# Three norms of a two-block transformer kernel: a shifted mean, embedding products moved ahead of their gate, and another order of the index projections

## The chip, the cores and the metric

The kernel runs on one core of a Trainium2 chip. The metric is the device time of one execution in microseconds (us), lower is better; shown are the median and the span of three runs. One further execution was recorded by the profiler; all rows below come from it.

## The reference, cut to what matters

Sequence 256 (T), width D = 2048, everything in float32. The first block (adaptive norms, latent attention beside a short convolution, a convolutional feed-forward part) ends in `rms_norm(x, g_final)`. The second block is

```python
def second_block(x, p, ...):
    for i in range(2):
        h = mixer_a(x, ...) if i == 0 else mixer_b(x, ...)
        x = layer_norm(ALPHA * x + h, ln_g[i], ln_b[i])
        x = x + (p[i] @ w_ple[i]) * sigmoid(x @ w_ple_gate[i])
    return x

def layer_norm(x, g, b):
    mu = mean(x)
    var = mean(square(x - mu))
    return (x - mu) * rsqrt(var + 1e-5) * g + b
```

`mixer_a` projects x to q, k, v, a gate, an index query iq (1024 columns), an index key ik (64) and index weights iw (16), chooses keys by the index scores and attends; `mixer_b` is a stick-breaking attention. Both end in a product with an output matrix w_o (2048 x 2048).

## The kernel before

Activations lie transposed: a tile is 128 features x 256 tokens, and the residual `X` is 16 such tiles [128, 16, 256] in SBUF. Weights stream from HBM in chunks of 128 x 2048 floats (1 MB); `schedule()` writes the order of all 342 chunks out by hand, and every engine walks that order. Products are made exact enough by a split in three: ScalarE copies a chunk to a rounded high part (`split(c)` on ScalarE, L376, three `HI` buffers), VectorE subtracts to get the low part (`split(c)` on VectorE, L872), and TensorE does high x high, high x low, low x high (`product`/`chunk`, all recorded under L1664). A chunk is 48 products 128x128x256. Its `HI` buffer is free for chunk c+3 when TensorE has ended chunk c. Four chunks make a group of 512 output columns, which gathers in one of two PSUM tiles `ACC[g % 2]`; a third PSUM tile, `AUX`, takes sums. SyncE issues the chunk loads, five `RAW` buffers ahead.

What the change touches:

- **The final norm of block one** (`n2`). When the last group of the down projection ends (phase `down2`), VectorE adds it to X (`residual`, L1296), ScalarE squares X (`norm_squares`, L621), VectorE sums the squares over the tiles (`part_total`, L996), TensorE sums over the partitions with a matrix of ones (`wide_totals`, into `AUX`), VectorE, ScalarE and VectorE form 1/root (`variance` L1002, `root` L438, L1005), and `normed` (L1026, L1028) with `hi_quarter` (L421) and `lo_quarter` (L1014) makes X and its high and low parts by quarters of four tiles. Then phase `ikw` (2 chunks: index key and weights, 96 products) starts; its loop waits for both parts of all quarters of a chunk. VectorE forms rotation angles (`angles`), ScalarE their sines, both ahead of the split of further chunks. Phase `iq` (8 chunks) follows, then `k_a`, `v_a`, `q_a`, `gate_a`, `o_a`.
- **The layer norms** (`ln0` after `o_a`, `ln1` after `o_b`). `o_a` is 16 chunks. `add_alpha` (L1555) does X = ALPHA X + ACC by group. After the last group: `early_sum`, `last_sum` (L1563, L1570) sum X over tiles, TensorE sums over partitions, VectorE subtracts the mean (L1581), ScalarE squares (L433), VectorE sums (L996), TensorE sums, root, `normed` (L1026, L1029), high and low parts. Then 16 chunks `pgate{i}`, whose groups ScalarE reads with Sigmoid into `U` (L514).
- **The embedding** (`ple{i}`): two chunks, four groups, 96 products, after the gate. VectorE multiplies U by each group (L1606) and, when all four are done, adds U to X by quarters (L1611). After `ple0` X is split again (L421, L1014) for `k_b`; after `ple1` X is stored in four DMAs (L323).

The feed-forward norm `nf` of block one is already done in another form: the squares of tiles 0 to 11 are summed early, those of the last four go straight to the ones product tile by tile, and scale and root are one instruction per tile (L1272, L613, L1278).

Of the kernel before, what the change touches and what calls it, by code (L numbers as in the profile page):

```python
# [13 lines left out]
P = 128  # L14
T = 256
# [47 lines left out]
def schedule():  # L63
# [93 lines left out]
def two_blocks(nc, stream, ada_stream, vecs, consts, x_t, ctx_t, p_t, positions, out):  # L157
# [60 lines left out]
    SEL = place("selector", [P, 8])  # L218
    CC = R2[:, :].rearrange("p (k t) -> p k t", t=T)
# [44 lines left out]
    def sem(name):  # L264
        if name not in sems:
# [4 lines left out]
    NORMS = {"nx": (2, 4), "nc": (2, 4), "nkv": (1, 1), "nq": (1, 1), "n2": (2, 4), "ln0": (2, 4),  # L270
             "ln1": (2, 4)}
# [14 lines left out]
    def since(name, n):  # L286
        s, before = step(name)
        return s, before + n

# [18 lines left out]
    with nc.Block() as block:  # L308
# [3 lines left out]
        def _(eng):  # L312
# [8 lines left out]
            for q in range(4):  # L321
                eng.wait_ge(sem("x2_full"), q + 1)
                eng.dma_start(out[:, 4 * q:4 * q + 4, :], X[:, 4 * q:4 * q + 4, :]).then_inc(sem("stored"), 16)  # L323
            eng.wait_ge(sem("stored"), 64)

        @block.gpsimd
        def _(eng):
# [3 lines left out]
            eng.memset(SEL[:, 3:4], 1.0).then_inc(sem("selector"), 1)  # L331

# [37 lines left out]
        def _(act):  # L370
# [245 lines left out]
            def norm_squares(name):  # L616

                end = PH["ikw"][1]
                for before, s in ((1, slice(0, 12)), (0, slice(12, 16))):
                    act.wait_ge(acc_free, end - before)  # L620
                    nc.scalar.activation(Y[:, s, :], X[:, s, :], ACT.Square).then_inc(step(name + "_sq")[0], 1)  # L621

            def norm(name, dst):
                root(name, T)
                hi_of(dst, AH, name + "_full", name + "_hi")

# [45 lines left out]
            def enter2():  # L672
                norm("n2", X)
                act.wait_ge(sem("angles"), 1)

                for i, (cos, sin) in enumerate(((COS2, SIN2), (COSI, SINI))):
                    r = Y[:, i, :]
                    nc.scalar.activation(cos[:, :], r, ACT.Abs).then_inc(sem("abs_angle"), 1)
                    nc.scalar.activation(sin[:, :], r, ACT.Sin).then_inc(sem("tables"), 1)
                for i, cos in enumerate((COS2, COSI)):  # L680
                    act.wait_ge(sem("abs_angle"), 2)
                    nc.scalar.activation(cos[:, :], cos[:, :], ACT.Sin, bias=con("half_pi"), scale=-1.0)\
                        .then_inc(sem("tables"), 1)
            pending[0] = enter2
            c0 = PH["ikw"][0]
            for j in range(2):
                split(c0 + j)
                if j == 0:
                    norm_squares("n2")
                if j == 1:  # L690
                    flush()
            phase("iq", 2)
# [8 lines left out]

            def gate_evac(name, d0, func):

                g0 = PH[name][1]

                def evac(gi):
                    act_evac(g0 + gi, U[:, gi * 4 + d0:gi * 4 + d0 + 4, :], func=func)
                return evac
# [30 lines left out]
            def mixer(tag, k, v, q, gate, early, attend):  # L739
# [3 lines left out]
                split(c0)  # L743
                split(c0 + 1)
                flush()
# [46 lines left out]
            def layer_norm(i):  # L792
                def f():
                    squares(f"ln{i}", X, Y, ready=f"ln{i}_centred")
                    root(f"ln{i}", T)
                    hi_of(X, AH, f"ln{i}_full", f"ln{i}_hi")
                return f

            def embed(i, then):
                phase(f"pgate{i}", 4, evac=gate_evac(f"pgate{i}", 0, ACT.Sigmoid))  # L800
                c0 = PH[f"ple{i}"][0]
                split(c0)
                flush()
                split(c0 + 1)
                pending[0] = then

            phase("o_a", 4, then=layer_norm(0), done=4)
            embed(0, lambda: hi_of(X, AH, "x1_full", "x1_hi"))
# [45 lines left out]
            phase("o_b", 4, then=layer_norm(1), done=4)  # L854
            embed(1, lambda: None)
# [3 lines left out]
        def _(dve):  # L859
# [498 lines left out]

            def angles():
# [16 lines left out]
            def enter2():  # L1376
                dve.wait_ge(acc_free, PH["ikw"][1])
                part_total("n2", 1, 12)

            def final_norm():  # L1380
                variance("n2", T, D, EPS)
                normed("n2", X, X, lambda k: vec("g_final", k), None, "a_ready")
                angles()
            c0, g0 = PH["ikw"]
            last = PH["down2"][1] + 3
            for j in range(2):
                split(c0 + j)
                if j == 0:
                    part_total("n2", 0, 12)
                    residual("down2", 5 * KD)(3)  # L1390
                    enter2()
                else:
                    final_norm()

            def ikw_evac():
                take(g0)
                V.tensor_copy(Y[:, 12, :], ACC[g0 % 2][:, 0, :])
                V.tensor_copy(R0[0:IH, 0:T], ACC[g0 % 2][0:IH, 1, :]).then_inc(acc_free, 1)
                V.engine_nop().then_inc(sem("ik"), 1)
            pending[0] = ikw_evac  # L1400
            phase("iq", 2, evac=copy_out("iq", Y, 4))
# [48 lines left out]
            def early_a(m, gk, gq):  # L1450
                if m == 1:
# [8 lines left out]
                if 2 <= m < 5:  # L1460
                    b = (2, 0, 1)[m - 2]
                    n = 4 if b < 2 else 1
                    turn_pairs(Y[:, 4 + 4 * b:4 + 4 * b + n, :], COSI[:, :], SINI[:, :], PERMI, n, "index_in")
# [47 lines left out]
            def mixer(tag, k, q, gate, out, early, attend):  # L1511
# [14 lines left out]
                split(c0)  # L1526
                split(c0 + 1)
                flush()
# [16 lines left out]
            def by_act(gi):  # L1545
                pass

            def add_alpha(name):
                g0 = PH[name][1]

                def evac(gi):
                    take(g0 + gi)
                    dve.wait_ge(acc_free, g0 + gi)
                    x = X[:, bass.ds(gi * 4, 4), :]
                    V.scalar_tensor_tensor(out=x, in0=x, scalar=ALPHA, in1=ACC[(g0 + gi) % 2][:, :, :],  # L1555
                                           op0=ALU.mult, op1=ALU.add).then_inc(acc_free, 1)
                return evac

            def early_sum(i):
                def f():  # L1560

                    dve.wait_ge(acc_free, PH[f"pgate{i}"][1] - 1)
                    V.tensor_reduce(RSTD[:, T:2 * T], X[:, 0:12, :].rearrange("p k t -> p t k"), AX.X, ALU.add)  # L1563
                return f

            def last_sum(i):
                def f():
                    n = f"ln{i}"
                    dve.wait_ge(acc_free, PH[f"pgate{i}"][1])
                    link(V.tensor_reduce(RSTD[:, 0:T], X[:, 12:16, :].rearrange("p k t -> p t k"), AX.X, ALU.add))  # L1570
                    V.engine_nop().then_inc(sem(n + "_sum"), 1)
                return f

            def layer_norm(i):
                def f():
                    n = f"ln{i}"
                    dve.wait_ge(sem(n + "_mean"), 1)
                    link(V.tensor_scalar(RSTD[:, T:2 * T], AUX[:, 1, 0:T], 1.0 / D, None, ALU.mult))
                    for q in range(4):
                        s = slice(4 * q, 4 * q + 4)  # L1580
                        V.tensor_tensor(X[:, s, :], X[:, s, :], wide_bcast(RSTD[:, T:2 * T], 4), ALU.subtract)\  # L1581
                            .then_inc(sem(n + "_centred"), 1)
                    dve.wait_ge(sem(n + "_centred"), 4)
                    part_total(n, 0, 8)
                    part_total(n, 1, 8)
# [704 lines left out]
```

## Time and profile before

| | us |
|---|---|
| median of 3 runs | 2480.45 |
| lowest, highest | 2479.01, 2482.07 |
| the profiled execution | 2482.17 |
| its span in the trace | 2480.4 |
| mean granted TensorE clock | 0.968 of full |

Busy shares of the span: TensorE 94%, its weight loads 87%, VectorE 61%, ScalarE 40%. The DMA engines moved 190 GB/s on average. The chain of work that ended last lies 82% on TensorE and 11% on VectorE. In a row of the timeline the first number is the start, the second the duration of the merged run of instructions; durations of neighbouring TensorE instructions overlap, since they are pipelined, so the pace of products is read from starts.

### The profile page before, as it was taken

Reading aid. Unit: us, or ns where it says so; the run is one execution under the profiler, and the core shown is the slowest. Engines: PE = TensorE matmul, PEld = TensorE weight load, DVE = VectorE, ACT = ScalarE, POOL = GpSimd, SP = SyncE. Lnnn points to the kernel's source line nnn. Section 1 sums busy time; section 2 is a strip of 40 time slices with the busy share of each in tenths; the row PEclk is TensorE's granted clock in tenths of the full one; section 3 lists DMA queues with packets and bytes.
Section 4 is the critical chain, followed back from the end, with each engine's and each line's share of the span. In section 5 each row is a group of like instructions: output and inputs, shape, how many; then the busy total and the mean of one; then the engine's idle time right before and its main releaser. Section 6 shows DMA issues by size and latency. Waiting matters only on the chain.

```text
span 2480.4 us, 39098 instructions
## 1 busy us (share of the span) xinstructions
PE 2321.6 (94%) x17514; PEld 2157.9 (87%) x17514; DVE 1507.5 (61%) x1652; ACT 993.6 (40%) x922; POOL 59.0 (2%) x111
## 2 busy tenths in 40 slices
PE   6979999998999999999998799999959899999688
PEld 1249878898999999999998799899959899999688
DVE  2167777787877546554566678665474545545664
ACT  1033534434444334443443343445334336653232
POOL 1100000000000000000000000000000000000000
PEclk9989989999999999999999899999979899999899
DMA  9746855685776545554555354334525354335333
GB/s 387 282 159 234 302 224 206 231 315 184 297 264 221 194 179 185 187 183 178 184 187 187 119 183 157 125 127 158 187 85 187 141 185 150 120 138 185 136 136 119
DMA packets 64808, 471.84 MB, mean 190 GB/s; under 512 B 7200, under 2 KB 7200, under 8 KB 8192
## 3 DMA queue, kind: packets, MB, share of 16 engines
q1 hardware_dynamic: 50400, 365.65, 40.4%
q0 software_dynamic: 14096, 101.59, 10.9%
q8 instruction: 138, 2.26, 0.4%
q10 hardware_dynamic: 144, 2.10, 0.2%
q14 instruction: 30, 0.25, 0.0%
HBM read 467.21 MB, written 2.10 MB: 189 GB/s over the span
## 4 chain that ended last, share of the span: by engine, by line
PE 82%; DVE 11%; DMA 2%; ACT 2%; issue 2%; ACTq 0%; POOL 0%; DVEq 0%; POOLq 0%
PE acc L1664 71%; PE aux L1664 10%; DMA ada_raw<-ada_stream 2%; DVE lo L872 2%; ACT hi L376 1%; DVE ada_acc L892 1%; DVE rstd L996 1%; DVE rstd L1005 0%; DVE rstd L1563 0%; DVE x L1581 0%; DVE x L1611 0%; DVE x L1026 0%; DVE rstd L989 0%; PE aux L1854 0%; DVE rope_scratch L1411 0%
## 5 line engine op out<-in xcount | busy, mean ns | idle before, releaser
L872 DVE TENSOR_TENSOR lo<-raw,hi 128x2048 fp32r<-128x2048 f32 x342 | 782.2, 2290 | 699.0 <-ACT hi L376 698.7
L376 ACT ACTIVATE hi<-raw 128x2048 fp32r<-128x2048 f32 x342 | 652.8, 1913 | 840.0 <-PE acc L1664 825.3
L1664 PE MATMUL acc<-act_hi,hi 128*128 128x256 f32 x4464 | 618.9, 290 | 58.4 <-DVE u_lo L1014 18.1
L1664 PEld LDWEIGHTS acc<-act_hi,hi 128*128 128x128 f32 x4464 | 576.2, 196 | 74.7 <-issue 68.6
L1664 PE MATMUL acc<-act_lo,hi 128*128 128x256 f32 x4464 | 599.2, 285 | 4.0 <-DVE act_lo L1014 4.0
L1664 PE MATMUL acc<-act_hi,lo 128*128 128x256 f32 x4464 | 595.4, 283 | 0.0
L1664 PEld LDWEIGHTS acc<-act_lo,hi 128*128 128x128 f32 x4464 | 567.3, 194 | 4.3 <-DVE act_lo L1014 4.3
L1664 PEld LDWEIGHTS acc<-act_hi,lo 128*128 128x128 f32 x4464 | 563.3, 193 | 0.0
L892 DVE SCALAR_TENSOR_TENSOR ada_acc<-ada_raw,silu_c,ada_acc 128x512 f32<-128x512 f32 x224 | 153.7, 746 | 8.1 <-DMA ada_raw<-ada_stream 7.7
L1664 PE MATMUL aux<-ada_raw,silu_c 128*2 128x512 f32 x256 | 113.8, 599 | 20.4 <-DMA ada_raw<-ada_stream 20.4
L1664 PEld LDWEIGHTS aux<-ada_raw,silu_c 128*2 128x2 f32 x256 | 20.8, 85 | 107.0 <-issue 93.3
L1664 PE MATMUL acc<-u_hi,hi 128*128 128x256 f32 x688 | 89.8, 283 | 0.0
L1664 PE MATMUL acc<-u_lo,hi 128*128 128x256 f32 x688 | 89.7, 283 | 0.0
L1664 PE MATMUL acc<-u_hi,lo 128*128 128x256 f32 x688 | 89.7, 283 | 0.0
L1664 PEld LDWEIGHTS acc<-u_lo,hi 128*128 128x128 f32 x688 | 85.7, 192 | 0.0
L1664 PEld LDWEIGHTS acc<-u_hi,lo 128*128 128x128 f32 x688 | 85.7, 192 | 0.0
L1664 PEld LDWEIGHTS acc<-u_hi,hi 128*128 128x128 f32 x688 | 85.7, 192 | 0.0
L639 ACT ACTIVATE y<-acc,vectors 128x256 f32<-128x256 f32 x86 | 41.7, 565 | 79.9 <-PE acc L1664 79.9
L335 POOL DMA_DIRECT2D ada_raw<-ada_stream x96 | 51.1, 533 | 704.5 <-DVE ada_acc L892 588.5
L1312 DVE SCALAR_TENSOR_TENSOR y<-acc,vectors,y 128x255 f32<-128x255 f32 x86 | 35.6, 476 | 49.3 <-ACT y L639 49.3
L1664 PE MATMUL aux<-rstd,ones 128*128 128x256 f32 (+1 forms) x30 | 13.9, 595 | 44.4 <-DVE rstd L996 29.8
L1664 PEld LDWEIGHTS aux<-rstd,ones 128*128 128x128 f32 x30 | 7.4, 279 | 49.1 <-DVE rstd L996 31.4
(297 smaller groups left out, 1616.7 us busy)
## 6 DMA issues: line engine op xcount, KB each, us to landing
raw<-stream SPq DMA_DIRECT2D x342, 1024.0 KB, 4.8
ada_raw<-ada_stream POOLq DMA_DIRECT2D x96, 1024.0 KB, 5.7
x<-x_t SPq DMA_DIRECT2D x1, 2048.0 KB, 9.3
ctx<-ctx_t SPq DMA_DIRECT2D x1, 2048.0 KB, 16.2
x<-x_t ACTq DMA_DIRECT2D x1, 2048.0 KB, 9.0
out<-x SPq DMA_DIRECT2D x4, 512.0 KB, 2.9
p_raw<-p_t POOLq DMA_DIRECT2D x1, 512.0 KB, 4.8
consts<-consts SPq DMA_DIRECT2D x1, 385.5 KB, 19.2
```

The costliest lines, as they stand in the source:

```text
L335: eng.dma_start(ADA[slot][:, :], ada_stream[n]).then_inc(ada_full[slot], 16)
L376: nc.scalar.activation(HI[c % NH][:, :], RAW[c % NR][:, :], ACT.Copy).then_inc(hi_done, 1)
L639: nc.scalar.activation(Y[:, i, :], ACC[(base[0] + gi) % 2][:, t, :], ACT.Identity, scale=VV[:, bass.ds(w + 1, 1)], bias=VV[:, bass.ds(w + ...
L872: V.tensor_tensor(LO[c % NR][:, :], RAW[c % NR][:, :], HI[c % NH][:, :].bitcast(F32), ALU.subtract)\
L892: V.scalar_tensor_tensor(out=a, in0=w, scalar=s, in1=a, op0=ALU.mult, op1=ALU.add)\
L996: ins = V.tensor_reduce(o, src.rearrange("p k t -> p t k"), AX.X, ALU.add)
L1312: ins = V.scalar_tensor_tensor(out=Y[:, i, 1:T], in0=acc[:, t, 0:T - 1], scalar=VV[:, bass.ds(w, 1)], in1=Y[:, i, 1:T], op0=ALU.mult, op1= ...
L1664: return TE.matmul(out, lhs, rhs, start=start, stop=stop, skip_group_check=True)
```

## The change

**Final norm and index projections.** `iq` comes ahead of `ikw` in the schedule. The norm takes the form that `nf` has. Chunks of `iq` start with their own quarter of the high part, and wait for the low part only at their second pass. `angles` and the sines move into `iq`; ScalarE, not VectorE, reads the groups of `iq`; `ikw` is a plain group, read at the start of `k_a`.

**Layer norms and embedding.** `ple{i}` comes ahead of `pgate{i}`. After two groups of `o` a mean over 1024 features is taken as `SHIFT` (two sums, and a product with ones after chunk 8 of `o`) and subtracted; the norm's sums are then taken of the shifted values, as mean and mean of squares, and VAR = E[y^2] - E[y]^2. The sums over partitions stand inside `ple`, after its first 12 products. Product and sum with the embedding are done with each gate group (`finished`), the last group in halves.

The schedule:

```diff
+    wide("iq", "w_in_a_2", 5120, 2)
     phase("ikw")
     group("w_in_a_2", [(6144, 6208), (6144, 6208)] + 8 * [(6208, 6224)], per=8)
-    wide("iq", "w_in_a_2", 5120, 2)
...
     def embed(i):
-        wide(f"pgate{i}", "w_ple_gate_2", 0, 4, layer=i)
         phase(f"ple{i}")
         for g in range(2):
             group("w_ple_2", [(1024 * g, 1024 * (g + 1))], range(2), layer=i, n_groups=2)
+        wide(f"pgate{i}", "w_ple_gate_2", 0, 4, layer=i)
```

VectorE at the final norm (`n2_scaled` is one instruction a tile in the form of L1272; ScalarE's `n2_high` and splits stand in the same order):

```diff
+            n2_scaled(0)
+            n2_scaled(1)
+            n2_low(0)
+            split(c0 + 2)
+            n2_scaled(2)
+            n2_low(1)
+            split(c0 + 3)
+            n2_scaled(3)
+            n2_low(2)
+            n2_low(3)
```

VectorE in the new `embed(i, o, nxt)`; c0 is the first chunk of `o`, so that 16 and 17 are `ple`, 18 to 33 `pgate`:

```diff
+                for n in range(2, 16):
+                    split(c0 + n + 2)
+                    if n in (4, 8):
...
+                        V.scalar_tensor_tensor(out=x, in0=x, scalar=ALPHA, in1=ACC[(go + g) % 2][:, :, :],
+                                               op0=ALU.mult, op1=ALU.add).then_inc(acc_free, 1)
+                        dve.wait_ge(acc_free, go + g + 1)
+                        total_of(RSTD[:, T * g:T * g + T], x, "ln_first")
+                    if n == 9:
+                        dve.wait_ge(*ln(i, "mean", 1))
+                        link(V.tensor_scalar(SHIFT, AUX[:, 0, 0:T], 1.0 / (D // 2), None, ALU.mult))
...
+                scaled(0)
+                scaled(1)
+                low(0)
+                split(c0 + 18)
+                scaled(2)
+                low(1)
+                split(c0 + 19)
+                scaled(3)
+                low(2)
+                low(3)
+
+                for n in range(18, 34):
+                    if n < 32:
+                        split(c0 + n + 2)
+                    elif nxt:
+                        split(PH[nxt][0] + n - 32)
+                    if n in (23, 27, 31):
+                        g = (n - 23) // 4
+                        dve.wait_ge(acc_free, gg + g + 1)
+                        finished(4 * g, 4 * g + 4)
```

Between them, by n: 9 and 10 subtract SHIFT from quarters 0 and 1 (128x1024 each); 10 and 11 form ALPHA X - SHIFT in quarters 2 and 3; 12 adds ACC to quarter 2; 13 sums the squares of tiles 0 to 7 (128x2048), 14 sums X in quarter 2, 15 its squares. Behind the loop ACC is added to quarter 3 in halves; then MEAN, its square, the variance and the reciprocal. `scaled(q)` subtracts MEAN from a quarter and multiplies its four tiles by gain and 1/root; `low` makes the low part tile by tile; `finished(a, b)` multiplies gate by embedding and adds the product and the norm's bias to X.

ScalarE in the same function, behind the root (`high` makes the high part by tiles, `embedded(g)` copies an embedding group to `U` and frees its ACC tile):

```diff
+                embedded(0)
+                high(0)
+                embedded(1)
+                split(c0 + 18)
+                high(1)
+                embedded(2)
+                split(c0 + 19)
+                high(2)
+                embedded(3)
+                high(3)
```

TensorE:

```diff
+                def shift(c):
+                    if c == c0 + 8:
+                        pe.wait_ge(*ln(i, "first", 2))
+                        mm(AUX[:, 0, 0:T], ONES[:, :], RSTD[:, 0:T], True, False)
+                        mm(AUX[:, 0, 0:T], ONES[:, :], RSTD[:, T:2 * T], False, True).then_inc(sem("ln_mean"), 1)
...
+                            if g == g0 and k == 0:
+                                sums()
```

`sums` is 5 products with ones on sums and tiles of X and 6 on sums and tiles of squares. For `k_b` the quarters of X are split as they become final. The output is stored in five DMAs, the last two of two tiles each.

## Rows read from the trace of the kernel before

**Rows 1.** The page, part 1: busy us (share), instructions.

```profile
PE 2321.6 (94%) x17514; PEld 2157.9 (87%) x17514; DVE 1507.5 (61%) x1652; ACT 993.6 (40%) x922; POOL 59.0 (2%) x111
```

**Rows 2.** Waits over the span: us in total, times, longest.

```profile
ACT hi L376 <- PE acc L1664: 825.3, 243, 9.0
DVE lo L872 <- ACT hi L376: 698.7, 241, 10.1
```

**Rows 3.** Timeline, one chunk of o_a: start, us, engine, line, instruction.

```profile
1804.96 2.08 PE L1664 MATMUL acc<-act_hi,hi 128*128 128x256 f32 x16
...
1805.22 1.92 ACT L376 ACTIVATE hi<-raw 128x2048 fp32r<-128x2048 f32 x1 [3.84 <-PE acc L1664]
...
1807.17 2.29 DVE L872 TENSOR_TENSOR lo<-raw,hi 128x2048 fp32r<-128x2048 f32 x1 [3.47 <-ACT hi L376]
```

**Rows 4.** Windows: stretch, length, busy us, PEclk, DMA share, GB/s.

```profile
596.00:601.00 5.00, 2.67 (x13) 1.71 (x11) 2.97 (x6) 1.29 (x3) 0.00 (x0) 1.00 0.59 211
...
1354.60:1373.90 19.30, 2.08 (x5) 1.21 (x5) 17.49 (x27) 7.72 (x7) 0.00 (x0) 0.59 0.16 55
...
1816.50:1846.80 30.30, 4.29 (x10) 2.35 (x8) 25.22 (x19) 6.58 (x5) 0.00 (x0) 0.54 0.09 35
...
2334.20:2364.40 30.20, 4.23 (x9) 2.34 (x8) 25.13 (x18) 6.58 (x5) 0.00 (x0) 0.56 0.10 35
```

**Rows 5.** Timeline around the final norm n2, to the start of k_a.

```profile
1353.00 1.60 PE L1664 MATMUL acc<-u_hi,lo 128*128 128x256 f32 x12
1354.79 1.65 DVE L1296 SCALAR_TENSOR_TENSOR x<-acc,ada,x 128x256 f32<-128x256 f32 x4
...
1385.42 1.28 ACT L679 ACT_TABLE_LOAD   x1
1386.71 0.42 ACT L679 ACTIVATE sin<-y 128x256 f32<-128x256 f32 x1
...
1436.62 2.08 PE L1664 MATMUL acc<-act_hi,hi 128*128 128x256 f32 x16
```

**Rows 6.** Timeline around the norm nf of block one.

```profile
596.90 1.65 DVE L1200 SCALAR_TENSOR_TENSOR x<-acc,ada,x 128x256 f32<-128x256 f32 x4
...
598.48 1.99 PE L1664 MATMUL aux<-y,ones 128*128 128x256 f32 x8 [1.80 <-ACT y L609]
...
603.20 3.25 DVE L1272 SCALAR_TENSOR_TENSOR y<-x,scales,rstd 128x256 f32<-128x256 f32 x8
603.72 3.30 ACT L613 ACTIVATE act_hi<-y,ada 128x256 fp32r<-128x256 f32 x8 [2.34 <-DVE y L1272]
...
605.57 3.75 PE L1664 MATMUL acc<-act_hi,hi 128*128 128x256 f32 x16 [5.10 <-ACT act_hi L613]
...
613.61 2.08 PE L1664 MATMUL acc<-act_hi,hi 128*128 128x256 f32 x16
```

**Rows 7.** Timeline from the end of o_a to the second chunk of k_b.

```profile
1814.56 2.08 PE L1664 MATMUL acc<-act_hi,lo 128*128 128x256 f32 x16
...
1821.68 1.93 DVE L1570 TENSOR_REDUCE rstd<-x 128x256 f32<-128x1024 f32 x1
...
1838.16 2.08 PE L1664 MATMUL aux<-rstd,ones 128*128 128x256 f32 x4 [12.36 <-DVE rstd L996]
...
1841.18 1.75 DVE L1005 RECIPROCAL rstd<-rstd 128x256 f32<-128x256 f32 x1 [0.48 <-ACT rstd L438]
1842.96 1.22 DVE L1026 TENSOR_TENSOR x<-x,rstd 128x1024 f32<-128x1024 f32 x1
...
1846.84 3.40 PE L1664 MATMUL acc<-act_hi,hi 128*128 128x256 f32 x16 [6.61 <-ACT act_hi L421]
...
1970.34 2.08 PE L1664 MATMUL acc<-act_hi,hi 128*128 128x256 f32 x16
```

**Rows 8.** Timeline from the end of o_b to the end.

```profile
2332.20 2.08 PE L1664 MATMUL acc<-act_hi,lo 128*128 128x256 f32 x16
...
2472.25 4.62 DVE L1611 TENSOR_TENSOR x<-x,u 128x1024 f32<-128x1024 f32 x4
```

More of the change, by code:

```diff
@@ L288, in since, with ln @@
         return s, before + n
+    LN_COUNTS = {"sq": 5, "hi": 16, "scaled": 16, "ready": 16, "first": 2, "mean": 1, "centred": 2, "begun": 2,
+                 "part": 3, "last": 2, "sums": 2, "var": 1, "std": 1, "gate": 2}
+    def ln(i, kind, n):
+        return sem("ln_" + kind), i * LN_COUNTS[kind] + n
     raw_full = [sem(f"raw_full{i}") for i in range(NR)]
@@ L614, in _ @@
                     .then_inc(sem("nf_hi"), 1)
[L616 to L625, printed above, removed]
             seen = [0]
@@ L684, in _ @@
[L684 to L692, printed above, removed]
+            c0, g0 = PH["iq"]
+            last = PH["down2"][1] + 3
+            act.wait_ge(acc_free, last)
+            nc.scalar.activation(Y[:, 0:12, :], X[:, 0:12, :], ACT.Square).then_inc(sem("n2_sq"), 1)
+            split(c0)
@@ new lines, in _, with n2_high @@
+            split(c0 + 1)
+            for i in range(2):
+                act.wait_ge(sem("x_summed"), 2 * i + 2)
+                s = slice(12 + 2 * i, 14 + 2 * i)
+                nc.scalar.activation(Y[:, s, :], X[:, s, :], ACT.Square).then_inc(sem("n2_sq"), 1)
+            root("n2", T)
+            def n2_high(q):
+                act.wait_ge(sem("n2_scaled"), 4 * q + 4)
+                nc.scalar.activation(AH[:, 4 * q:4 * q + 4, :], X[:, 4 * q:4 * q + 4, :], ACT.Copy)\
+                    .then_inc(sem("n2_hi"), 1)
@@ L790, in _ @@
             mixer("a", "k_a", "v_a", "q_a", "gate_a", early_a, attend_a)
[L792 to L805, printed above, removed]
@@ L809, in _ @@
+            embed(0, "o_a", "k_b")
             steps3 = [0]
@@ L853, in _ @@
             mixer("b", "k_b", "v_b", "q_bb", "gate_b", lambda m: None, attend_b)
-            phase("o_b", 4, then=layer_norm(1), done=4)
-            embed(1, lambda: None)
+            embed(1, "o_b", None)
         @block.vector
@@ L1357, in _, with n2_scaled, n2_low @@
                             res(g)
+            c0, g0 = PH["iq"]
+            last = PH["down2"][1] + 3
+            dve.wait_ge(sem("n2_sq"), 1)
+            V.tensor_reduce(RSTD[:, T:2 * T], Y[:, 0:12, :].rearrange("p k t -> p t k"), AX.X, ALU.add)\
+                .then_inc(sem("n2_ss"), 1)
+            split(c0)
+            split(c0 + 1)
+            take(last)
+            for t in range(4):
+                k = 12 + t
+                V.scalar_tensor_tensor(out=X[:, k, :], in0=ACC[last % 2][:, t, :],
+                                       scalar=MOD[:, 5 * KD + k:5 * KD + k + 1], in1=X[:, k, :],
+                                       op0=ALU.mult, op1=ALU.add).then_inc(sem("x_summed"), 1)
+            dve.wait_ge(sem("x_summed"), 4)
+            V.engine_nop().then_inc(acc_free, 1)
+            variance("n2", T, D, EPS)
+            def n2_scaled(q):
+                for k in range(4 * q, 4 * q + 4):
+                    V.scalar_tensor_tensor(out=X[:, k, :], in0=X[:, k, :], scalar=vec("g_final", k),
+                                           in1=RSTD[:, 0:T], op0=ALU.mult, op1=ALU.mult).then_inc(sem("n2_scaled"), 1)
+            def n2_low(q):
+                dve.wait_ge(sem("n2_hi"), q + 1)
+                s = slice(4 * q, 4 * q + 4)
+                V.tensor_tensor(AL[:, s, :], X[:, s, :], AH[:, s, :].bitcast(F32), ALU.subtract)\
+                    .then_inc(sem("a_ready"), 1)
             def angles():
@@ L1374, in angles @@
                 V.engine_nop().then_inc(sem("angles"), 1)
[L1376 to L1401, printed above, removed]
+            n2_scaled(0)
+            n2_scaled(1)
+            n2_low(0)
+            split(c0 + 2)
+            n2_scaled(2)
+            n2_low(1)
+            split(c0 + 3)
+            n2_scaled(3)
+            n2_low(2)
+            n2_low(3)
+            for m in range(2, 10):
+                split(c0 + m + 2)
+                if m == 4:
+                    angles()
             pairs_last = []
@@ L1543, in _ @@
             mixer("a", "k_a", "q_a", "gate_a", "out2", early_a, attend_a)
[L1545 to L1557, printed above, removed]
@@ L1574, in layer_norm @@
[L1574 to L1585, printed above, removed]
-                    variance(n, T, D, LN_EPS)
-                    normed(n, X, X, lambda k: vec("ln_g", KD * i + k), lambda k: vec("ln_b", KD * i + k),
-                           n + "_ready")
-                return f
@@ L1591, in _ @@
-            phase("o_a", 4, evac=add_alpha("o_a"), before=early_sum(0), first=last_sum(0),
-                  then=layer_norm(0), done=4)
-            def embed(i, then):
-                phase(f"pgate{i}", 4, evac=by_act)
-                c0, g0 = PH[f"ple{i}"]
-                split(c0)
-                split(c0 + 1)
-                flush()
-                def ple():
-                    dve.wait_ge(acc_free, g0)
-                    for g in range(4):
-                        take(g0 + g)
-                        s = slice(4 * g, 4 * g + 4)
-                        V.tensor_tensor(U[:, s, :], U[:, s, :], ACC[(g0 + g) % 2][:, :, :], ALU.mult)\
-                            .then_inc(acc_free, 1)
-                    for g in range(4):
-                        dve.wait_ge(acc_free, g0 + g + 1)
-                        s = slice(4 * g, 4 * g + 4)
-                        V.tensor_tensor(X[:, s, :], X[:, s, :], U[:, s, :], ALU.add)\
-                            .then_inc(sem("x1_full" if i == 0 else "x2_full"), 1)
-                ple()
-                pending[0] = then
@@ L1617, in _ @@
+            embed(0, "o_a", "k_b")
             strict = con("strict")
@@ L1652, in _ @@
             mixer("b", "k_b", "q_bb", "gate_b", "out3", lambda m, gk, gq: None, attend_b)
-            phase("o_b", 4, evac=add_alpha("o_b"), before=early_sum(1), first=last_sum(1),
-                  then=layer_norm(1), done=4)
-            embed(1, lambda: None)
-            flush()
+            embed(1, "o_b", None)
         @block.tensor
```

268 lines of the change are left out of this document (193 added, 75 removed).

## The prediction, as it was put on record

> **What bounds the kernel now.** I read the page first. TensorE is busy 94% of the span and VectorE 61% [rows 1]: on average TensorE sets the time. The waits agree: the longest are ScalarE waiting for TensorE to free a `HI` buffer, and VectorE waiting for ScalarE [rows 2]; both are ahead of the work, not behind. The timeline of one chunk shows the beat: TensorE starts a pass every 1.92 us, so a chunk takes 5.76; ScalarE starts its split 0.26 after the chunk boundary, VectorE follows at 2.21 and ends at 4.50 [rows 3]. What VectorE does besides has 5.76 - 2.29 = 3.47 us a chunk free.
>
> An average does not price a change in three places, so I went to the stretches where TensorE stands. At n2 it works 2.08 of 19.3 us, behind o_a 4.29 of 30.3, behind o_b 4.23 of 30.2, while VectorE works 17.5, 25.2 and 25.1 [rows 4]: there VectorE's serial chain is the bound, and the granted clock falls to 0.54 to 0.59, a mix of the levels 2.4 and 1.2 GHz. All three are on the path, and the change works in them.
>
> Three durations of before, each from the true end of the last product pass (start plus number of products times 0.12):
> - n2: 1353.00 + 12 x 0.12 = 1354.44 to the start of k_a at 1436.62: 82.2 us [rows 5]. Its products are 2 chunks ikw (96 x 0.12 = 11.5) and 8 chunks iq (46.1), so 24.6 are loss.
> - ln0: 1814.56 + 1.92 = 1816.48 to the second chunk of k_b at 1970.34: 153.9 us [rows 7].
> - ln1: 2332.20 + 1.92 = 2334.12 to the end at 2480.4: 146.3 us [rows 8].
>
> **The final norm after the change.** It takes nf's form, and nf is in the trace. From the first addition of the last group (596.90) to the first product behind the norm (605.57) are 8.67 us [rows 6]. The addition at n2 starts at 1354.79 [rows 5], which stays: the early square and reduction start earlier than before, and the splits c0 and c0+1 end by about 1354.6 by the beat of rows 3. One difference: the high part is one copy of a quarter, not four tiles. It waits for four scaled tiles (3.25 / 8 = 0.41 each), 1.2 us later than for one, but replaces four instructions; half of the 1.92 us copy of 128x2048 is 1.0, so the quarter is ready about 0.4 later than nf's. First product: 1354.79 + 8.67 + 0.4 = 1363.9. nf's first chunk took 613.61 - 605.57 = 8.04 instead of 5.76, as the clock was down [rows 6]: 2.3 lost. I checked the next chunks: VectorE's order puts low(2) at about 1379.5, when chunk 2 wants it; no wait, or tenths. The angles and sines now lie inside iq, and the split queued behind them on either engine is wanted two chunks later, so iq hides them; without that cover ScalarE's load and functions would come back, 1.28 + 4 x 0.42 = 3.0 [rows 5]. So k_a starts at 1363.9 + 2.3 + 46.1 + 11.5 = 1423.8, against 1436.6: gain 12.8 us.
>
> The key comes later than before, but VectorE reads it at step 0 of k_a, the index weights are turned at step 1, and the first index scores are wanted at step 5: nothing. The two group copies move from VectorE to ScalarE, both idle there; nothing.
>
> A rule of the Trainium skill would make this a little dearer: "ScalarE: Activation LUTs", What ACT_TABLE_LOAD costs, puts a change of table set at about 2.66 us, load and drain. In this trace the load takes 1.28 and the sine starts 1.29 after it began [rows 5]. The root's load stands here between the last square (ends about 1357.1) and the variance (about 1358.8): by the row it is hidden, by the page n2 would be 1.0 us dearer. The trace does not agree with the drain; I take the row.
>
> **The layer norms after the change**, from the end of o (zero):
> - 12 embedding products, 12 x 0.12 = 1.44, then 11 products with ones. Four of nf's (x8, two instructions a product) took 1.99 with the clock up, the pipelined end included; I take 0.48 each [rows 6]: 5.3. At 6.75 the sums stand. Their inputs come in time: VectorE's last reduction (1.93 [rows 7] behind a split) ends at 0.75, the two half additions at 1.4 and 2.05, squares at 2.7, TensorE wants them at 1.95, 2.9, 4.8.
> - From the start of the last ones product pair plus 2.08 to the first instruction behind the reciprocal: 1842.96 - 1840.24 = 2.7 [rows 7].
> - VectorE's chain to scaled(3): four quarters of one 128x1024 subtraction (1.22 + 0.04 link) and four tiles (1.62), 11.5; low(0), low(1), 3.3 (8 tiles at the same 0.41); two splits, 4.6: together 19.4. low and the splits are on this path; ScalarE's pieces fit between.
> - high's last tile, 0.4, then ScalarE's split of the third pgate chunk, 1.9.
> - Sum: 6.75 + 2.7 + 19.4 + 2.3 = 31.1: the third pgate chunk starts here. TensorE's own work would let it start at 1.44 + 5.3 + 10.1 + 2 x 5.76 = 28.4. So it waits 2.7 us, partly ahead of pgate (its first group needs embedded(2), about 18.5, against 16.8). Bounds of this term: 0 if VectorE's chain is 2.7 shorter, 5 if every quarter takes half a microsecond more in waits.
> - 14 chunks more, 80.6: pgate ends at 111.7.
> - In o itself the shift costs: VectorE starts step 8 at 4.5 of the beat, adds 1.2, sums 1.93, and is done 2.0 us after chunk 8 ends; TensorE waits there, and makes two ones products, 1.0. Price 3.0; bounds 1.0 (sum early) and 4.0. Step 13 (128x2048 sum, 3.6) is the fullest step, 2.29 + 3.6 = 5.9 of 5.76, and step 14 has room. Nothing more.
> - pgate thus ends at 111.7 + 3.0 = 114.7, counted from an end of o without the shift.
>
> Behind ln0 k_b's quarters 0 to 2 are ready and the fourth is wanted 17 us later, so k_b follows at once, its second chunk 5.8 later: 120.5 against 153.9, gain 33.4. The multiplications and additions (about 2.9 a group) fit in the 3.47; uncovered, the one of the last quarter would cost 4 to 6 us there.
>
> Behind ln1 the last quarter is the tail: sigmoid of a half about 0.8 (estimate: a quarter of 1.92 and some start), then twice 1.5 on VectorE (one half-wide product 0.65, two tiles 0.82): 3.9. Before, 2472.25 + 4.62 = 2476.87 to 2480.4 is 3.5 for store and end [rows 8]. End at 114.7 + 7.4 = 122.1 against 146.3, gain 24.2.
>
> **Sum:** 12.8 + 33.4 + 24.2 = 70.4 us. 2480.4 - 70.4 = 2410.0 in the span. The profiled execution is 1.7 above the median of the runs, and the span almost equals that median (2480.45), so the runs should show 2410.
>
> **Rivals.**
> (a) The cover has holes: VectorE's steps in o run over (step 13 is full already), or TensorE restarts at the lower clock behind the waits in ple and pgate. Each restart costs 2.3 as at nf, each overrun chunk about 1; two restarts, 3 us of waits at each layer norm and 2 at n2: 2410 + 12.6 = 2423. For it: tightly set waits. Against: at nf TensorE stood 1.8 us (596.7 to 598.48) and the window shows 1.00 [rows 4].
> (b) The index order gives nothing, because iq waits for quarters as ikw did or the later key holds k_a: then the 12.8 stay, 2423. Against it: five chunks of distance.
> (c) The other side: slower. The new places where TensorE stops briefly (chunk 8, pgate's first and third chunk) keep the clock at 1.2 GHz in what follows. A chunk at that level costs 5.76 more (pass 3.4 to 3.75 instead of 1.92 [rows 6, 7]); from 70.4 / 5.76 = 12.2 such chunks on the kernel is slower. All 32 of pgate would give 2410 + 184 = 2594. Against it: behind 30 us of standstill TensorE was back at full pace after one pass (1846.84, 3.40) or two. The skill has such a case, "TensorE: Matmul & The Clock Gate", A second HAM failure mode: psum-queue depth-cycling, where short idles between groups make the clock go up and down; this trace, with a new ACC tile every group and the clock at 1.00 across nf's 1.8 us of standstill [rows 4], does not bear it out.
> (d) It does what it says and ScalarE or VectorE have more slack than I think: no wait at pgate, shift's sum early: 2410 - 2 x (2.7 + 2.0) = 2401.
>
> **How the numbers follow.** Forecast with its bounds (2405 to 2417) 0.68, (a) 0.14, (b) 0.04, (c) 0.02, (d) 0.10, something else of either kind 0.02. The time is that of the forecast, 2410. The range 2402 to 2424 takes in (a), (b) and nearly all of (d). A measurement here tells 0.2%, 5 us, from no change. Faster by more 0.97, within 0.01, slower 0.02.
>
> **What would show it.** In the profile of the changed kernel: first iq product about 9.1 us behind the last group's first addition and no gap between iq, ikw and k_a; a gap of 2 us behind chunk 8 of o_a and o_b; pgate's third chunk 31 us behind the end of o; no gap between pgate0 and k_b; 7.4 us from the last product to the end. Wrong it goes if the weights' low parts come late in o, if pgate waits for more than its third chunk, or if the granted clock stays below 1.00 past the first chunks.

## The result and the profile after

| | us |
|---|---|
| before, median (4 runs) | 2480.94 (2479.01 to 2482.07) |
| after, median (4 runs) | 2409.26 (2408.65 to 2411.0) |
| ratio | 0.9713, 95% interval 0.9701 to 0.9724 |
| span of the profiled execution, before and after | 2480.4, 2406.9 |

The forecast was 2410.0. One of the nine executions of the kernel before that were made beside after_again (a second set of runs of the changed kernel, below) took 3176.47 us at a mean granted clock of 0.673 and is left out of the ratios.

The page's first part after shows TensorE with 2 us less work than before in a span 73.5 us shorter (beside [rows 1]):

```profile
PE 2319.2 (96%) x17556; PEld 2157.5 (90%) x17556; DVE 1505.5 (63%) x1703; ACT 1008.8 (42%) x965; POOL 59.0 (2%) x112
```

The final norm in the timeline after (start, duration, engine, instruction):

```profile
1350.21 1.60 PE L1780 MATMUL acc<-u_hi,lo 128*128 128x256 f32 x12
...
1351.85 1.66 DVE L1421 SCALAR_TENSOR_TENSOR x<-acc,ada,x 128x256 f32<-128x256 f32 x4
...
1354.19 1.28 ACT L446 ACT_TABLE_LOAD   x1
1355.48 0.42 DVE L1054 TENSOR_SCALAR rstd<-aux 128x256 f32<-128x256 f32 x1 [1.97 <-PE aux L1780]
1355.93 0.42 ACT L446 ACTIVATE rstd<-rstd 128x256 f32<-128x256 f32 x1 [0.46 <-DVE rstd L1054]
...
1361.08 3.75 PE L1780 MATMUL acc<-act_hi,hi 128*128 128x256 f32 x16 [5.64 <-ACT act_hi L683]
...
1368.93 2.08 PE L1780 MATMUL acc<-act_hi,hi 128*128 128x256 f32 x16
...
1420.77 2.08 PE L1780 MATMUL acc<-act_hi,hi 128*128 128x256 f32 x16
```

Read against [rows 5]: the down projection ends at 1350.21 + 1.44 = 1351.65 and k_a starts at 1420.77, 69.1 us later, where it took 82.2. The first iq product starts 9.2 us behind the first addition (forecast 9.1). The first chunk takes 7.85 us, and from there seven chunks of 5.76 and the 96 products of ikw at 0.12 fill the time to k_a exactly, so there is no other gap. The root follows the variance at once: its table load ended at 1355.47, before the variance began.

Behind o_a, timeline after, from the mean's sum to the second chunk of k_b:

```profile
1758.51 2.08 PE L1780 MATMUL acc<-act_hi,lo 128*128 128x256 f32 x16
1759.09 1.21 DVE L1661 SCALAR_TENSOR_TENSOR x<-x,acc 128x1024 f32<-128x1024 f32 x1
1760.33 1.97 DVE L1627 TENSOR_REDUCE rstd<-x 128x256 f32<-128x1024 f32 x1
...
1762.36 1.13 PE L1780 MATMUL aux<-rstd,ones 128*128 128x256 f32 x4 [1.78 <-DVE rstd L1627]
...
1803.64 0.28 PE L1780 MATMUL acc<-p_hi,hi 128*128 128x256 f32 x1
...
1821.65 2.17 PE L1780 MATMUL acc<-act_hi,hi 128*128 128x256 f32 x16 [1.17 <-ACT u L522]
...
1834.33 1.94 PE L1780 MATMUL acc<-act_hi,hi 128*128 128x256 f32 x14 [0.92 <-ACT hi L384]
...
1915.07 2.08 PE L1780 MATMUL acc<-act_hi,hi 128*128 128x256 f32 x16
...
1920.83 2.08 PE L1780 MATMUL acc<-act_hi,hi 128*128 128x256 f32 x16
```

TensorE stands 1.78 us behind chunk 8 of o_a, works through the embedding from 1803.64 (with one wait of 0.15), waits 1.17 for the ACC tile that embedded(2) frees and 0.92 for the high part of pgate's third chunk, and goes from pgate into k_b (1915.07) without a gap. What was a block of 30 us with 4 us of work [rows 4, 7] is four small gaps. These gaps count from the modelled end of the last product; counted from its start plus 0.12, as the prediction counts, the stand behind chunk 8 is 1.93 and the three waits behind o_a are 2.7 together.

Behind o_b, and the end:

```profile
2287.19 2.08 PE L1780 MATMUL acc<-act_hi,lo 128*128 128x256 f32 x16
...
2319.80 2.17 PE L1780 MATMUL acc<-act_hi,hi 128*128 128x256 f32 x16 [0.91 <-ACT hi L384]
...
2398.61 2.08 PE L1780 MATMUL acc<-act_hi,lo 128*128 128x256 f32 x16
2400.73 1.09 ACT L856 ACTIVATE u<-acc 128x512 f32<-128x512 f32 x2 [15.30 <-PE acc L1780]
...
2403.60 0.88 DVE L1650 SCALAR_TENSOR_TENSOR x<-x,vectors,u 128x256 f32<-128x256 f32 x2
```

**Where the 73.5 us of the two spans come from**, each stretch between the same two events: n2 82.2 to 69.1 (13.1); end of o_a to second chunk of k_b 153.9 to 117.2, less the 2.9 by which o_a itself became longer (33.8); end of o_b to the end 146.3 to 117.8, less 4.5 in o_b (24.0). That is 70.9. Another 2.8 lie ahead of n2 (the down projection ends at 1354.44 before and 1351.65 after), where no instruction was changed; in the eleven experiments below that have the changed norm and so the same code up to there, it ends between 1351.9 and 1354.9. So the 2.8 lie within the scatter of single executions, and the medians, 71.7 apart, have less of it.

### The profile page after: what moved, and what is told of

It is laid out like the page before. It is cut to its first block, busy times and chain, and to the rows that moved or that the text cites. A ratio compares the mean times of both kernels' runs of the same rounds, so it can differ in the third digit from the quotient of the medians.

```text
span 2406.9 us, 39294 instructions
## 1 busy us (share of the span) xinstructions
PE 2319.2 (96%) x17556; PEld 2157.5 (90%) x17556; DVE 1505.5 (63%) x1703; ACT 1008.8 (42%) x965; POOL 59.0 (2%) x112
## 4 chain that ended last, share of the span: by engine, by line
PE 83%; DVE 10%; DMA 2%; ACT 2%; issue 2%; POOL 0%; DVEq 0%; ACTq 0%; POOLq 0%
PE acc L1780 72%; PE aux L1780 11%; DMA ada_raw<-ada_stream 2%; DVE lo L924 2%; ACT hi L384 1%; DVE ada_acc L944 1%; DVE x L1633 0%; DVE x L1630 0%; DVE rstd L1041 0%; DVE rstd L1057 0%; PE aux L1970 0%; DVE act_lo L1640 0%; ACT probs L727 0%; DVE rope_scratch L1479 0%; DVE rstd L1316 0%
## 5 line engine op out<-in xcount | busy, mean ns | idle before, releaser
L1780 PE MATMUL acc<-act_hi,hi 128*128 128x256 f32 x4464 | 610.8, 289 | 36.5 <-DVE u_lo L1066 18.1
L1780 PE MATMUL acc<-act_lo,hi 128*128 128x256 f32 x4464 | 591.8, 284 | 0.0
L1780 PE MATMUL acc<-act_hi,lo 128*128 128x256 f32 x4464 | 588.8, 283 | 0.0
L727 ACT ACTIVATE probs<-probs,columns 128x256 f32<-128x256 f32 x32 | 16.0, 501 | 73.5 <-DVE columns L1568 73.5
```

Of the source, the lines that this page charges most:

```text
L727: ins = nc.scalar.activation(s, s, ACT.Exp, bias=COL[:, 4 * (h % 2) + qt:4 * (h % 2) + qt + 1], accum_out=COL[:, 4 * (h % 2) + 2 + qt:4 * ...
L1780: return TE.matmul(out, lhs, rhs, start=start, stop=stop, skip_group_check=True)
```

## The experiments

Medians are compared on runs beside each other where they were made together: of the changed kernel there are two medians, 2409.26 and 2407.94 (after_again). The kernel before was run in every set, with medians from 2480.9 to 2482.0. Beside key_first, three_orders, all_orders and finish_tail only the kernel before was run, on another chip than after_again's, so their distance to the changed kernel is less certain than their ratio to before, by about 1 us (the medians of before in the two sets are 2481.2 and 2482.0).

**index_part and norms_part: do the parts add up?** The first is the kernel before with the final norm, iq/ikw and the readers of the index groups as changed; the second is the changed kernel with these as before.

The schedule of index_part has the new order of the index phases and the old one of gate and embedding; norms_part has it the other way round:

```python
    wide("iq", "w_in_a_2", 5120, 2)
    phase("ikw")
    group("w_in_a_2", [(6144, 6208), (6144, 6208)] + 8 * [(6208, 6224)], per=8)
...
    def embed(i):
        wide(f"pgate{i}", "w_ple_gate_2", 0, 4, layer=i)
        phase(f"ple{i}")
```

> The kernel before with the final norm in its new form and iq ahead of ikw, the two layer norms as before. By the prediction's sum the gain is 12.8 us (2480.9 to about 2468): k_a starts 69.4 us behind the end of the last down group instead of 82.2. The rival (the order of the index phases gives nothing, or the late key holds k_a) expects 2479 to 2481. If the gain of the whole came from the layer norms alone, the same.

> The changed kernel with the final norm and the index phases as before, the layer norms and the embedding as changed. By the sum 33.4 + 24.2 = 57.6 us less than before: about 2423. If the two parts help or hinder each other, index_part and norms_part do not add up to the 71.7 us of the whole; the theory that the three places are independent expects them to, within 2 us.

index_part: 2467.64, ratio to before 0.9948 (0.9933 to 0.9963), 13.5 us less. norms_part: 2423.12, 0.9766 (0.9751 to 0.978), 58.0 us less. Sum 71.5, and the whole is 71.7: the two parts are independent within the scatter. In index_part's trace k_a starts 69.2 us behind the down projection. The rival that the index side gives nothing is out. How the 58.0 us divide between the earlier sums (`SHIFT`) and the embedding put ahead of its gate, no run shows: these two were not run apart.

**key_first: norm's form or order of the phases?** The changed kernel with ikw ahead of iq, and the readers of their groups moved with them. On TensorE:

```diff
-            phase("iq", 2, ready=by_quarters("n2_hi", "a_ready"))
             c0, g0 = PH["ikw"]
-            group(c0, g0, AH, AL, ks=(8, 8), tiles=2, width=256)
+            group(c0, g0, AH, AL, ks=(8, 8), tiles=2, width=256,
+                  ready=lambda j: (since("n2_hi", 2 * j + 2), (sem("a_ready"), 2 * j + 2)))
+            phase("iq", 2)
```

> The changed kernel with ikw ahead of iq again, the norm n2 in its new form (VectorE reads the group of ikw in step 3, ScalarE the second iq group in step 0 of k_a). A chunk of ikw takes eight tiles of X, so it wants two quarters. Theory from the changed kernel's rows: it starts 1.6 us later (high part of quarter 1), its second pass waits about 3 us for low(1), its second chunk about 3 us for high(3): 6.5 to 7.6 us more than the changed kernel (2415 to 2417), so that about half of index_part's 13.5 us is the order and half the norm's form. Rival: the form makes the whole gain and the order none: 2408 to 2410.

2424.35, ratio to before 0.977 (0.9756 to 0.9783): 15.1 us above the changed kernel's 2409.26, twice what I expected. The timeline of its TensorE:

```profile
1365.17 3.57 PE L1778 MATMUL acc<-act_hi,hi 128*128 128x256 f32 x16 [7.22 <-ACT act_hi L683]
1371.92 3.62 PE L1778 MATMUL acc<-act_lo,hi 128*128 128x256 f32 x16 [3.19 <-DVE act_lo L1435]
...
1384.61 3.75 PE L1778 MATMUL acc<-act_hi,hi 128*128 128x256 f32 x16 [7.15 <-ACT act_hi L683]
```

The later start (about 1.6) and the 3.19 us for low(1) are as expected. The second chunk waits 7.15, not 3: scaled(3) and high(3) stand behind split(c0 + 3) in both queues, that split needs the `HI` buffer of ikw's first chunk, and this chunk was itself late. Then the second chunk starts at the lower clock again (3.75 a pass). From the end of the down projection to the end of the second chunk behind it are 38.1 us, against 23.0 in the changed kernel: that is the whole difference of 15.1. So the norm's form with these splits between its quarters needs the order iq first. With the last split behind high(3) the 7.15 and the second restart should go, and by my estimate some 6 of the 15.1 us remain; that was not run. What is shown is that the form with these splits, without the order, gives nothing (norms_part, with the old form and the old order, took 2423.12), and not how much the order alone would give.

**double_sum: what a longer stand costs.** VectorE makes the sum of step 8 twice.

```diff
+                        if n == 8:
+                            link(V.tensor_reduce(SUM8, x.rearrange("p k t -> p t k"), AX.X, ALU.add))
                         total_of(RSTD[:, T * g:T * g + T], x, "ln_first")
```

> The changed kernel with the sum of step 8 made twice on VectorE, so that TensorE stands about 2.0 us longer behind chunk 8 of o_a and o_b (3.8 instead of 1.8). A theory without the clock expects 2 x 2.0 = 4.0 us more than the changed kernel (2413). The theory that a stand of this length brings the clock down to 1.2 GHz expects up to 2.3 more at each place, 4 to 8.6 us in all (2413 to 2418), and the granted clock below 1.00 behind both stands. The rival of a lasting fall expects hundreds of us.

2414.33, ratio to before 0.9735 (0.972 to 0.9749), 5.1 to 6.4 us above the changed kernel. TensorE now stands 3.70 us at both places. Windows of double_sum, the stand and what follows (length, busy us by engine, granted clock, DMA share, GB/s):

```profile
1763.50:1767.30 3.80, 0.18 (x2) 0.00 (x0) 3.77 (x3) 1.91 (x1) 0.00 (x0) 1.00 0.64 220
1767.30:1772.00 4.70, 4.62 (x22) 4.46 (x23) 3.78 (x4) 0.00 (x0) 0.00 (x0) 0.64 0.13 49
2250.80:2254.60 3.80, 0.19 (x2) 0.00 (x0) 3.77 (x3) 1.91 (x1) 0.00 (x0) 0.78 0.57 211
2254.60:2260.00 5.40, 5.31 (x22) 4.96 (x23) 3.85 (x4) 0.00 (x0) 0.00 (x0) 0.53 0.11 46
```

In this execution the clock falls at both stands and TensorE is back at its full pace after one pass. 2 x 1.9 us of stand is 3.8; the rest is the lower clock. The profiled execution was the slowest of the four (2417.83, the others 2413.80 to 2414.47), so the others may have lost less to it. The rival of a lasting fall would have cost hundreds and is out, also at twice the stand.

**early_sum: can the stand go?** VectorE adds and sums group 1 ahead of the split of step 8.

```diff
                 for n in range(2, 16):
-                    split(c0 + n + 2)
+                    if n != 8:
+                        split(c0 + n + 2)
                     if n in (4, 8):
...
                         total_of(RSTD[:, T * g:T * g + T], x, "ln_first")
+                    if n == 8:
+                        split(c0 + n + 2)
```

> The changed kernel with VectorE's step 8 of o_a and o_b (add group 1, sum it) ahead of the split of that step, not behind it. Theory: the group has ended 2.2 us before ScalarE's high part is there, so VectorE adds and sums while it waited before; the sum stands 3.5 us after the chunk boundary instead of 7.7, and TensorE's stand of 1.8 us behind chunk 8 goes at both places, with 1.1 us of lower clock behind the second: 3.6 to 4.7 us less (about 2405). Rival: the low part of the chunk comes later and TensorE waits for that instead, or the wait returns at the ones product: no gain.

and of the changed kernel beside it:

> The changed kernel once more, as the level that the three kernels beside it are compared with: 2409 +- 2.

2403.88 against 2407.94 for the changed kernel beside it, ratio to before 0.9688 (0.9676 to 0.9701) against 0.9704 (0.9692 to 0.9717): 4.1 us less by the medians. The two intervals overlap, as both carry the scatter of the kernel before, but the slowest of its five runs (2406.44) is below the fastest of the changed kernel's five (2407.63). The timeline shows the mechanism; the ones product follows the pass without a wait:

```profile
1758.31 1.22 DVE L1662 SCALAR_TENSOR_TENSOR x<-x,acc 128x1024 f32<-128x1024 f32 x1 [1.46 <-PE acc L1783]
...
1759.56 2.05 DVE L1627 TENSOR_REDUCE rstd<-x 128x256 f32<-128x1024 f32 x1
...
1761.52 2.28 DVE L924 TENSOR_TENSOR lo<-raw,hi 128x2048 fp32r<-128x2048 f32 x1
1761.94 2.08 PE L1783 MATMUL acc<-act_hi,lo 128*128 128x256 f32 x16
1763.86 1.02 PE L1783 MATMUL aux<-rstd,ones 128*128 128x256 f32 x4
```

**scalar_order, three_orders: who sets pgate's third chunk?** scalar_order reorders ScalarE; three_orders moves VectorE's split too. ScalarE's edit:

```diff
                 embedded(1)
+                embedded(2)
                 split(c0 + 18)
                 high(1)
-                embedded(2)
                 split(c0 + 19)
                 high(2)
                 embedded(3)
+                split(c0 + 20)
                 high(3)
```

(The split moved is the third pgate chunk's; the loop that follows leaves it out.) VectorE's, in three_orders alone:

```diff
                 low(2)
+                split(c0 + 20)
                 low(3)
```

> The changed kernel with another order on ScalarE behind the root: embedded(2) directly behind embedded(1), and the split of the third pgate chunk ahead of high(3). Theory: TensorE's two waits there (1.2 us for the ACC tile, 0.9 for the high part of the third chunk) shrink to some tenths: 2 x 1.5 to 2 x 2.1 us less (2405 to 2406). Rival: VectorE's chain to scaled(3) is the bound as the prediction's sum has it, its low part of the third chunk or the low part of the last quarter comes late, and TensorE waits the same time one pass later: 2409.

> scalar_order with VectorE's split of the third pgate chunk ahead of low(3) too. In scalar_order TensorE waited 1.5 us for that low part in each layer norm, after the waits of before were gone. Theory: that wait goes and nothing takes its place, 2 x 1.5 us less than scalar_order, which with its own 2 x 0.7 makes 4.4 less than the changed kernel: about 2404. Rival: low(3) now comes too late for the fourth chunk and the wait moves on again: 2408.

scalar_order: 2409.0 against 2407.94, no gain that can be told. three_orders: 2402.55, ratio to before 0.9684 (0.9671 to 0.9697), 5.4 us below 2407.94; all its runs (2402.38 to 2404.84) lie below all those of the changed kernel. The waits of TensorE from chunk 8 of o_b to the third chunk of pgate1 (who waits for whom: us in total, times, longest), first in the changed kernel:

```profile
PE aux L1780 <- DVE rstd L1627: 1.8, 1, 1.8
PE acc L1780 <- ACT u L522: 1.3, 2, 1.2
PE acc L1780 <- ACT hi L384: 0.9, 1, 0.9
```

then in scalar_order:

```profile
PE aux L1781 <- DVE rstd L1628: 1.8, 1, 1.8
PE acc L1781 <- DVE lo L925: 1.5, 1, 1.5
PE acc L1781 <- ACT u L522: 0.2, 1, 0.2
```

and in three_orders:

```profile
PE aux L1782 <- DVE rstd L1628: 1.8, 1, 1.8
PE acc L1782 <- ACT u L522: 0.2, 1, 0.2
```

With 2.0 us of the waits for ScalarE gone, TensorE waited 1.5 for VectorE's low part of the same chunk instead. Only with that split moved too does the wait go. Of scalar_order's two views the rival was right, of three_orders' the theory: what bound was VectorE's queue in the order low(3), split, and not the length of its chain, which is the same in all three. The 0.5 us a layer that scalar_order should still have gained do not show in its median, and three_orders gained more than the 2 x 2.0 us of these waits; both differences are about as large as the scatter.

**both_orders and all_orders.** early_sum with scalar_order, and with three_orders.

> Both reorderings. If they are independent, the sum of the two gains: 6.5 to 9 us less than the changed kernel (2401 to 2403).

> three_orders and early_sum together: 4.1 and 4.4 us less than the changed kernel, if they add: about 2400.

both_orders: 2403.31, 0.9682 (0.9668 to 0.9695). all_orders: 2401.08, 0.9675 (0.9662 to 0.9689). In all_orders one wait is left to TensorE in that stretch, 0.2 us. By the medians it is 7 to 8 us below the changed kernel, where the gains of early_sum and three_orders against 2407.94 add to 9.5. It has the lowest median of all versions run, and all its runs (2399.57 to 2401.70) lie below all of three_orders'. The 2401 to 2403 expected of both_orders was nearly met by early_sum's gain alone: in its trace TensorE waits 1.5 us for VectorE's low part in each layer, as in scalar_order.

**finish_late, finish_tail: is product and sum by group worth its place?** In the second layer the first three pieces of `finished` are made behind the last split, or when the last group's first sigmoid is there.

```diff
-                    if n in (23, 27, 31):
+                    if nxt and n in (23, 27, 31):
...
+                if not nxt:
+                    dve.wait_ge(*ln(i, "gate", 1))
+                    for g in range(3):
+                        finished(4 * g, 4 * g + 4)
                 for h in range(2):
```

(This is finish_tail; in finish_late the wait is for the group's own evacuation, `acc_free`.)

> The changed kernel, but in the second layer VectorE makes product and sum with the first three gate groups only behind the last split, not with each group. Theory: the three pieces of 2.9 us, hidden in pgate1 before, come onto the tail: 8.6 us more (2418), less what of it still runs while TensorE works on the last chunk (VectorE is free 4.5 us into it, so up to 1.3 per chunk and some 3 to 5 us in all): 2413 to 2418. Rival: the tail is set by the stores and the last group alone, then 2409 to 2410.

> The changed kernel, but in the second layer VectorE makes product and sum with the first three gate groups only when the last group's first sigmoid is there. (finish_late let them run in the shadow of the last two chunks.) Theory: three pieces of 2.9 us and the stores behind them come onto the tail: 8.6 us more than the changed kernel, 2417 to 2418. Rival: only the last stores count and the pieces overlap with something: 2409 to 2412.

finish_late: 2408.58, nothing. My expectation counted wrongly: behind the last split there are no more splits, so VectorE is free for nearly three chunks of TensorE's, and the three pieces ran from 2387.65 to 2396.3 while TensorE worked on till 2400.5. finish_tail: 2418.71, ratio 0.9746 (0.9733 to 0.976), 9.5 to 10.8 us more, of which 8.5 are the three pieces; the rest no trace explains. In its timeline the last addition ends 12.3 us behind the sigmoid's start, where the changed kernel takes 3.75; the three pieces of 2.85 stand between:

```profile
2399.90 1.09 ACT L856 ACTIVATE u<-acc 128x512 f32<-128x512 f32 x2 [15.30 <-PE acc L1784]
2400.53 1.23 DVE L1648 TENSOR_TENSOR u<-u 128x1024 f32<-128x1024 f32 x1 [13.60 <-ACT u L856]
2401.79 1.67 DVE L1650 SCALAR_TENSOR_TENSOR x<-x,vectors,u 128x256 f32<-128x256 f32 x4
2403.38 1.22 DVE L1648 TENSOR_TENSOR u<-u 128x1024 f32<-128x1024 f32 x1
...
2411.30 0.88 DVE L1650 SCALAR_TENSOR_TENSOR x<-x,vectors,u 128x256 f32<-128x256 f32 x2
```

So what counts is that the pieces end before the last group does, not that each stands with its own group.

## Why the prediction was right, by its own steps

| step | predicted | measured |
|---|---|---|
| n2, gain | 12.8 | 13.1 (index_part: 13.5) |
| first iq product behind the first addition | 9.07 | 9.23 |
| lost to the clock there | 2.3 | 2.1 |
| both layer norms, gain | 57.6 | 57.8 (norms_part: 58.0) |
| stand behind chunk 8 | 2.0 each | 1.9, 1.9 |
| shift in o_a, o_b | 3.0 each | 2.9, 4.5 |
| third pgate chunk behind the end of o | 31.1 | 30.7, 30.7 |
| waits of TensorE in that stretch, by starts | 2.7 | 2.7, 2.7 |
| pgate's end behind the end of o | 111.7 | 111.4, 111.4 |
| last product to the end | 7.4 | 6.4 |
| all | 70.4 | 71.7 |

- **The final norm** went by nf's precedent within 0.2 us. The table load cost nothing here, as the row had it: it took 1.28 from 1354.19 to 1355.47, and the root started at 1355.93, 0.03 behind the variance's end. With the 2.66 us for load and drain of the Trainium skill, "ScalarE: Activation LUTs", What ACT_TABLE_LOAD costs, it could by estimate not have started before 1356.85.
- **The layer norms.** The sum stands: from the first instruction behind the reciprocal to the end of scaled(3) VectorE took 19.0 us (forecast 19.4), and ScalarE's last high tile and split another 2.4 (forecast 2.3). But the chain sets pgate's third chunk only because both engines have its split queued behind the last quarter; with the split moved, in three_orders, the chunk no longer waits. The fullest step, 13, had a sum of 3.88 instead of 3.6 and made VectorE's next split 0.25 us late, without a wait of TensorE.
- **The shift.** The stand was as forecast at both places, 1.93. What was missing is the clock: at the second place the two ones products took 0.7 us and the pass behind them 0.9 us longer than at the first, 1.6 in all. Rival (a) named such restarts at 2.3; one happened, at two thirds of the price.
- **Luck.** In the second layer norm the shift was 1.5 us dearer than the sum has it and the tail 1.0 cheaper; that the gain came within 0.2 of the forecast 24.2 is mostly these two misses cancelling.
- **The tail** was 1.0 too dear: I took store and end from before, 3.5 behind the last addition. Now the last two stores are 256 KB, 2.0 us from issue to landing on the page, where the 512 KB stores of before took 2.9, and the end comes 2406.9 - 2404.48 = 2.4 behind the last addition.
- **Rival (c)**, a lasting lower clock, is out: in the trace after, the clock fell at one short stand, but TensorE was back at its full pace after one pass, and so it was after the 3.7 us stands of double_sum. The case in the Trainium skill, "TensorE: Matmul & The Clock Gate", A second HAM failure mode: psum-queue depth-cycling, has the clock going up and down with frequent short idles; in these traces a short stand cost at most the ones products and one pass at a slower pace, and no up and down followed.
- **Rival (b)** is out by index_part. key_first lands at its 2423, because there the order is taken away and the form alone gives nothing.
- **Rival (d)** needed other queue orders than the change has; all_orders reached its 2401 with them.

## What to carry to other kernels

A norm in the middle of a kernel is a serial chain through three engines; its price is read where the matrix engine stands. Independent products laid into it (here 96, and the next phase by quarters), with part of the sums taken earlier, brought two blocks of 30 us down to waits of 2.7 us each, at the price of a stand of 1.9 us in the phase before. When the big gap is closed, the small ones lie in the order of each engine's queue: look for an instruction whose input has long been there behind one that still waits, as the sum of step 8 behind a split, and move both engines' parts together, since moving one only moves the wait. A cover that is not yet full also takes late work for nothing, so a piece need not stand with its producer, only ahead of the end.

## What the runs showed of the hardware

A stand of the same 1.78 us left the clock at 1.00 at one place and not at the other in one execution of the changed kernel. The ones products in o_a and o_b and the passes behind them, then windows around them (length, busy us by engine, granted clock, DMA share, GB/s):

```profile
1763.14 2.26 PE L1780 MATMUL acc<-act_hi,hi 128*128 128x256 f32 x16
1765.24 2.08 PE L1780 MATMUL acc<-act_lo,hi 128*128 128x256 f32 x16
...
2246.24 2.01 PE L1780 MATMUL aux<-rstd,ones 128*128 128x256 f32 x4 [1.78 <-DVE rstd L1627]
...
2247.69 3.19 PE L1780 MATMUL acc<-act_hi,hi 128*128 128x256 f32 x16
2250.71 2.08 PE L1780 MATMUL acc<-act_lo,hi 128*128 128x256 f32 x16
```

```profile
1762.40:1765.00 2.60, 2.60 (x18) 2.50 (x19) 2.38 (x2) 0.19 (x1) 0.00 (x0) 1.00 0.86 353
...
2246.20:2250.00 3.80, 3.76 (x15) 3.41 (x15) 3.47 (x3) 0.27 (x1) 0.00 (x0) 0.55 0.60 250
```

By starts the ones products took 1763.14 - 1762.36 = 0.78 us at the first place and 1.45 at the second, and the pass behind them 2.10 and 3.02: 1.6 us more. Eight profiles have this stand at both places (after, after_again, scalar_order, three_orders, norms_part, key_first, finish_late, finish_tail). In fourteen of the sixteen cases ones products and pass went as at the first place; in two, behind chunk 8 of o_b in the changed kernel and in key_first, they took 1.6 us more. So a stand of this length costs its own time and, in some cases, 1.6 us more; what decides it no run shows. In double_sum's profile, with 3.7 us, the same products and pass took 1.5 us more at the first place and 2.3 at the second.
